# Softmax attention of a two-block transformer kernel: the last gate unit in halves through exp and ln, meta rows in a buffer of their own, the row maximum in two parts, transpositions between the scores

## The reference

```python
def gqa_block(q_blk, k, v):
    s = jnp.einsum('bkgqd,bksd->bkgqs', q_blk, k).astype(jnp.float32) * (HEAD_DIM ** -0.5)
    p = jax.nn.softmax(s, axis=-1)
    return jnp.einsum('bkgqs,bksd->bkgqd', p.astype(v.dtype), v)
...
        a_out = attention_branch(q, k, v, q_norm_g[i], k_norm_g[i], cos, sin, n_tok) * jax.nn.silu(a_gate)
```

## Time and profile before

| | us |
|---|---|
| median of 3 runs | 2239.23 |
| lowest and highest | 2237.02, 2241.11 |
| the profiled execution, its own time | 2239.75 |
| its span in the profile | 2238.0 |
| TensorE busy | 2123.8 |
| VectorE busy | 1104.5 |
| ScalarE busy | 831.3 |
| GpSimd busy | 746.5 |

### The profile page before, as it was taken

How to read it: one execution, slowest core, us unless ns; L and a number is a source line. 1 busy time by engine, 2 the same in 40 slices (tenths; PEclk the granted TensorE clock), 3 DMA queues, 4 the chain that set the end, 5 groups by cost and what they waited for, 6 DMA issues and landing times.

```text
span 2238.0 us, 27665 instructions
## 1 busy us (share of the span) xinstructions
PE 2123.8 (95%) x10545; PEld 1752.9 (78%) x10545; DVE 1104.5 (49%) x1483; ACT 831.3 (37%) x1482; POOL 746.5 (33%) x660
## 2 busy tenths in 40 slices
PE   5899998999998999999999999989999999999996
PEld 4687887999776778787877888868888888878785
DVE  7347656787434276766656743442222223221523
ACT  5133226888323264554545532431222122111212
POOL 3222141222232422222322334223333333366662
PEclk8999998999999999999999999999999999999998
DMA  5031130010132211111212443421111111132432
GB/s 171 26 123 52 48 94 27 10 48 10 55 113 81 66 58 52 53 61 52 79 42 80 155 141 124 132 76 47 47 47 47 47 47 47 47 113 94 148 106 76
DMA packets 142923, 164.68 MB, mean 74 GB/s; under 512 B 7092, under 2 KB 109000, under 8 KB 142824
## 3 DMA queue, kind: packets, MB, share of 16 engines
q1 hardware_dynamic: 118663, 98.10, 14.4%
q10 hardware_dynamic: 24160, 65.23, 8.3%
HBM read 133.94 MB, written 29.36 MB: 73 GB/s over the span
## 4 chain that ended last, share of the span: by engine, by line
PE 83%; DVE 10%; ACT 3%; issue 2%; DMA 1%; ACTq 0%; POOL 0%; DVEq 0%; POOLq 0%
PE psum L660 18%; PE psum L662 18%; PE psum L661 18%; PE psum L973 14%; PE psum L876 3%; PE psum L887 3%; PE psum L906 1%; PE psum L907 1%; PE psum L1010 1%; PE psum L908 1%; DVE softplus_part L2103 1%; PE psum L994 1%; DVE xn L1814 1%; PE psum L995 1%; PE psum L1027 1%
## 5 line engine op out<-in xcount | busy, mean ns | idle before, releaser
L557 POOL TENSOR_TENSOR w_ring<-w_staging,zero 128x8 fp32r<-128x8 f32 x172 | 44.3, 258 | 1227.6 <-PE psum L662 758.1
L560 POOL TENSOR_TENSOR w_ring<-w_staging,w_ring 128x1024 fp32r<-128x1024 f32 (+1 forms) x172 | 444.9, 2587 | 14.4
L973 PE MATMUL psum<-h,w_ring 128*128 128x512 f32 x1728 | 433.6, 401 | 0.7 <-ACT v L1489 0.7
L973 PEld LDWEIGHTS psum<-h,w_ring 128*128 128x128 f32 x1728 | 317.2, 190 | 67.6 <-ACT v L1489 1.1
L660 PE MATMUL psum<-ffn_in,w_ring 128*128 128x512 f32 x672 | 265.8, 395 | 0.0
L662 PE MATMUL psum<-ffn_in,w_ring 128*128 128x512 f32 x672 | 264.5, 394 | 0.0
L661 PE MATMUL psum<-ffn_in,w_ring 128*128 128x512 f32 x672 | 264.2, 393 | 0.0
L2236 DVE SCALAR_TENSOR_TENSOR up_buf<-psum,vectors,up_buf 128x1023 f32<-128x1023 f32 x44 | 56.5, 1283 | 308.2 <-ACT up_buf L1710 308.2
L558 POOL TENSOR_SCALAR w_ring<-w_staging 128x1016 fp32r<-128x1016 f32 (+1 forms) x172 | 183.8, 1069 | 0.0
L662 PEld LDWEIGHTS psum<-ffn_in,w_ring 128*128 128x128 f32 x672 | 126.1, 188 | 30.4
L661 PEld LDWEIGHTS psum<-ffn_in,w_ring 128*128 128x128 f32 x672 | 126.4, 188 | 29.0
(11 more groups left out here) (277 smaller groups left out, 4495.5 us busy)
## 6 DMA issues: line engine op xcount, KB each, us to landing
w_staging<-in_w_in SPq DMA_DIRECT2D x58, 512.0 KB, 3.8
w_staging<-in_w_up SPq DMA_DIRECT2D x44, 512.0 KB, 3.8
w_staging<-in_w_down SPq DMA_DIRECT2D x44, 512.0 KB, 3.2
w_staging<-in_w_out SPq DMA_DIRECT2D x16, 512.0 KB, 3.8
scratch_gates<-gate_out ACTq DMA_DIRECT2D x32, 256.0 KB, 2.3
merge_gates<-scratch_gates ACTq DMA_DIRECT2D x16, 512.0 KB, 4.5
x_again<-scratch_x ACTq DMA_DIRECT2D x16, 512.0 KB, 4.5
xin<-in_x ACTq DMA_DIRECT2D x8, 512.0 KB, 3.3
```

What stands on the lines that cost most here:

```text
L560: pool.tensor_tensor(lo[:, 0:width], WS[:, s, 0:width], plain(hi[:, 0:width]), ALU.subtract).then_inc(S["w_split"], 1)
L973: ins = pe.matmul(mix_bank(h), (sl if x == 2 else sh)[:, P * k:P * k + P], ml if x == 1 else mh, start=m == 0, stop=m == UNIT // 2 - 1)
```

## The change

- The last gate unit is made in halves: for each half of the tokens ScalarE takes exp of minus the value, ln of one plus that, and exp of minus that (the sigmoid from functions of the table that the softmax uses), into a buffer gate_e3 of its own. The first half is done in step 1 ahead of its exp, the second at the end of step 3. VectorE multiplies halves in steps 1 and 4. TensorE waits for the first half before attend of step 3 and for the second before that of step 5. The store goes out in step 5; only the load for head 6 waits for it. The sigmoid and both table loads of step 2 go.
- The copy in place behind each gate's product on VectorE goes; a store waits for the product.
- Meta rows of the transposed probabilities get a buffer probs_t_meta outside u. GpSimd clears it once the queries are all transposed. The split of chunk C_OUT+3 moves behind the meta rows of step 1.
- The maximum is taken over banks 0 and 1, then over bank 2, then the smaller of the two negatives by a third instruction on 128x1 elements.
- TensorE's step becomes: scores of banks 0 and 1, transpositions of group 0, scores of bank 2, transpositions of groups 1 and 2, attend.

```diff
@@ -280,7 +280,7 @@
         ZERO = at("zero", [P, 8], c0 + 688)
-        NB = at("minus_max", [P, 2], c0 + 424)
+        NB = at("minus_max", [P, 6], c0 + 424)
         IDR = at("ident_r", [P, P], c0 + 432, F32R)
@@ -340,7 +340,9 @@
         OT = at("attended", [P, 4, PAIR], T0 + 3624)
-        PT = at("probs_t", [P, 2, KTILES, 4 * P], R1, F32R)
+        PT = at("probs_t", [P, 2, TT, 4 * P], R1, F32R)
+        PTM = at("probs_t_meta", [P, 4 * P], T0 + 4648, F32R)
+        GE3 = at("gate_e3", [P, N_TOK], T0 + 5168)
         MIXA = at("mixed_a", [P, 2, 4, N_TOK], R1 + 9216, F32R)
@@ -365,7 +367,7 @@
         CAUSALR = at("causal_raw", [P, P], c1 + 2056)
-        ONE = at("one", [P, 1], c0 + 416)
+        ONE = at("one", [P, 2], c0 + 416)
@@ -560,8 +562,9 @@
+            pool.memset(ONE[:, 1:2], 1.0).then_inc(S["zero_set"], 1)
             pool.memset(ZERO[:, :], 0.0).then_inc(S["zero_set"], 1)
-            pool.wait_ge(S["zero_set"], 1)
+            pool.wait_ge(S["zero_set"], 2)
             peeled = C_KV + 4
@@ -591,7 +594,8 @@
-            run(peeled, C_OUT + 4, 1)
+            run(peeled, C_OUT + 3, 1)
+            pool.wait_ge(S["w_split"], C_OUT + 3)
@@ -607,8 +611,8 @@
-            pool.wait_ge(S["w_used"], C_OUT)
-            pool.memset(plain(PT[:, 0, TT, :]), 0.0).then_inc(S["pt_zero"], 1)
+            pool.wait_ge(S["pr_t"], KTILES + TT)
+            pool.memset(plain(PTM[:, :]), 0.0).then_inc(S["pt_zero"], 1)
             pool.wait_ge(S["pt_zero"], 1)
@@ -617,9 +621,12 @@
                     pool.wait_ge(S["o_lo"], (i - 10) // 2 + 1)
-                pool.tensor_scalar(PT[META_VLO:META_VLO + META, 0, TT, t], plain(PT[0:META, 0, TT, t]), 1.0, 0.0,
+                pool.tensor_scalar(PTM[META_VLO:META_VLO + META, t], plain(PTM[0:META, t]), 1.0, 0.0,
                                    ALU.mult, ALU.add).then_inc(S["pt_meta"], 1)
                 pool.wait_ge(S["pt_meta"], i + 1)
+                if i == 1:
+                    run(C_OUT + 3, C_OUT + 4, 1)
+                    pool.wait_ge(S["w_split"], C_OUT + 4)
                 if i >= 6 and i % 2 == 0:
@@ -724,6 +731,8 @@
                             ins.then_inc(S["w_used"], 1)
+                        elif c == C_AGATE + 3 and k == KT - 1:
+                            ins.then_inc(S["gate3_half"], 1)
                         if between is not None:
@@ -866,20 +875,21 @@
-            def scores(i):
+            def scores(i, parts=range(3)):
                 h, t = divmod(i, TT)
-                for b in range(3):
+                for b in parts:
                     if i:
...
                                         k2[:, h // GROUP, KPART * b:KPART * (b + 1)], start=x == 0, stop=x == 1)
-                ins.then_inc(S["sc_mm"], 1)
-
-            def turn_probs(i):
+                    if b:
+                        ins.then_inc(S["sc_half" if b == 1 else "sc_mm"], 1)
+
+            def turn_probs(i, groups=range(3)):
                 pe.wait_ge(S["sc_exp"], 3 * i + 3)
-                for g in range(3):
+                for g in groups:
                     if i:
@@ -907,7 +917,7 @@
                 if part:
-                    pe.matmul(dst, VV[0:META_ROWS, TT, g, 0:P], PT[0:META_ROWS, 0, TT, PAIR * (p % 2):PAIR * (p % 2) + PAIR],
+                    pe.matmul(dst, VV[0:META_ROWS, TT, g, 0:P], PTM[0:META_ROWS, PAIR * (p % 2):PAIR * (p % 2) + PAIR],
                               start=False, stop=True).then_inc(S["av_mm"], 1)
@@ -921,10 +931,16 @@
                 if i < HEADS * TT:
-                    scores(i)
+                    scores(i, range(2))
                 if i <= HEADS * TT:
-                    turn_probs(i - 1)
+                    turn_probs(i - 1, range(1))
+                if i < HEADS * TT:
+                    scores(i, range(2, 3))
+                if i <= HEADS * TT:
+                    turn_probs(i - 1, range(1, 3))
                 if i == 3:
+                    pe.wait_ge(S["gate_half"], 1)
+                elif i == 5:
                     settle(fm=U_AGATE + 4)
@@ -1359,8 +1375,21 @@
+            def a_gate_half(h):
+
+                if h:
+                    act.wait_ge(S["w_used"], C_AGATE + 4)
+                else:
+                    act.wait_ge(S["gate_stored"], 96)
+                    act.wait_ge(S["zero_set"], 2)
+                    act.wait_ge(S["gate3_half"], 1)
+                e = GE3[:, FW * h:FW * h + FW]
+                link(act.activation(e, PB[:, 2 * A_GATE_PAIRS[3] + h, :], ACT.Exp, scale=-1.0))
+                link(act.activation(e, e, ACT.Ln, bias=ONE[:, 1:2]))
+                act.activation(e, e, ACT.Exp, scale=-1.0).then_inc(S["gate3_sig"], 1)
+
             def store_a_gate(f):
-                act.wait_ge(S["gate_out"], 4 + f + 1)
+                act.wait_ge(S["fm_free"], U_AGATE + f + 1)
                 act.dma_start(scratch["a_gate"][P * f:P * f + P, :], GE2[:, f % 2, :]).then_inc(S["gate_stored"], 16)
@@ -1376,6 +1405,8 @@
                 r = DH * (h % 2)
+                if h == 6 and c == 0:
+                    act.wait_ge(S["gate3_stored"], 16)
                 act.dma_start(AG[r:r + DH, b % 2, :], scratch["a_gate"][DH * h:DH * h + DH, FW * c:FW * c + FW])\
@@ -1386,11 +1417,11 @@
                     act.wait_ge(S["pt_mm"], n + 1)
-                    rows = P if g < 2 else META
-                    kts = slice(4 * g, min(4 * g + 4, KTILES))
-                    act.activation(PT[0:rows, 0, kts, P * t:P * t + P],
-                                   PB[0:rows, 3 + g, 0:P * (4 if g < 2 else 1)].rearrange("p (k n) -> p k n", n=P),
-                                   ACT.Copy).then_inc(S["pt_hi"], 1)
+                    if g == 2:
+                        act.activation(PTM[0:META, P * t:P * t + P], PB[0:META, 5, 0:P], ACT.Copy).then_inc(S["pt_hi"], 1)
+                    else:
+                        act.activation(PT[:, 0, 4 * g:4 * g + 4, P * t:P * t + P],
+                                       PB[:, 3 + g, :].rearrange("p (k n) -> p k n", n=P), ACT.Copy).then_inc(S["pt_hi"], 1)
@@ -1409,15 +1440,15 @@
             for i in range(HEADS * TT):
+                if i == 1:
+                    a_gate_half(0)
                 if i == 2:
+                    act.wait_ge(S["w_used"], C_OUT)
                     act.wait_ge(S["pt_zero"], 1)
                     probs_hi(0)
-                    a_gate(3)
-                    load_tables()
-                if i == 4:
-                    store_a_gate(3)
                 if i == 5:
-                    act.wait_ge(S["gate_stored"], 112)
+                    act.wait_ge(S["fm_free"], U_AGATE + 4)
+                    act.dma_start(scratch["a_gate"][3 * P:4 * P, :], GE3[:, :]).then_inc(S["gate3_stored"], 16)
                     load_a_gate(0)
@@ -1428,6 +1459,8 @@
                     probs_hi(i - 1, range(2, 3))
+                if i == 3:
+                    a_gate_half(1)
                 if i >= 5 and i % 2:
@@ -1994,8 +2027,12 @@
                 v.tensor_tensor(e, pair(A_GATE_PAIRS[f]), e, ALU.mult).then_inc(S["fm_free"], 1)
-                v.wait_ge(S["fm_free"], 4 + f + 1)
-                v.tensor_scalar(e, e, 1.0, None, ALU.mult).then_inc(S["gate_out"], 1)
+
+            def a_gate_half(h):
+
+                e = GE3[:, FW * h:FW * h + FW]
+                v.wait_ge(S["gate3_sig"], h + 1)
+                v.tensor_tensor(e, PB[:, 2 * A_GATE_PAIRS[3] + h, :], e, ALU.mult).then_inc(S["fm_free" if h else "gate_half"], 1)
@@ -2006,31 +2043,37 @@
                 for g in groups:
-                    rows = P if g < 2 else META
-                    kts = slice(4 * g, min(4 * g + 4, KTILES))
                     v.wait_ge(S["pt_hi"], 3 * i + g + 1)
-                    lo = PT[:, 1, kts, P * t:P * t + P] if g < 2 else PT[META_LO:META_ROWS, 0, kts, P * t:P * t + P]
-                    v.tensor_tensor(lo,
-                                    PB[0:rows, 3 + g, 0:P * (4 if g < 2 else 1)].rearrange("p (k n) -> p k n", n=P),
-                                    plain(PT[0:rows, 0, kts, P * t:P * t + P]), ALU.subtract).then_inc(S["pt_lo"], 1)
+                    if g == 2:
+                        v.tensor_tensor(PTM[META_LO:META_ROWS, P * t:P * t + P], PB[0:META, 5, 0:P],
+                                        plain(PTM[0:META, P * t:P * t + P]), ALU.subtract).then_inc(S["pt_lo"], 1)
+                    else:
+                        kts = slice(4 * g, 4 * g + 4)
+                        v.tensor_tensor(PT[:, 1, kts, P * t:P * t + P], PB[:, 3 + g, :].rearrange("p (k n) -> p k n", n=P),
+                                        plain(PT[:, 0, kts, P * t:P * t + P]), ALU.subtract).then_inc(S["pt_lo"], 1)
...
                 if p == 0:
-                    v.wait_ge(S["gate_stored"], 112)
+                    v.wait_ge(S["gate_stored"], 96)
                 if p >= 4:
...
             for i in range(HEADS * TT):
+                first, last = (NB[:, 2 + 2 * (i % 2) + x:3 + 2 * (i % 2) + x] for x in range(2))
```

(14 more changed lines are left out.)

4 lines of the change are left out of this document (2 added, 2 removed).

## The result

| us | before | after |
|---|---|---|
| median of 5 runs each | 2239.23 | 2227.63 |
| lowest and highest | 2237.02, 2243.26 | 2225.14, 2229.91 |
| the profiled execution | 2239.75 | 2228.94 |
| its span | 2238.0 | 2227.1 |
| scores of step 2 start | 336.65 | 335.99 |

The account below looks back on a forecast made before the run. TensorE, busy 95% of the span, bounds the kernel; only its idle and slowed time in the softmax stage can change. Entry 9.6 plus steady 1.5 make 11.1 off the profiled 2239.75: about 2228.5 us, range 2222.5 to 2236, chance .42.

Parts of the forecast that it names:

- The entry: Start of the softmax stage: scores of step 5 at 349.19 instead of 358.79, a gain of 9.6 us.
- The steady gain: Softmax steps after the entry: 29 pairs of steps, each slightly shorter, 1.5 us gained, bounds 4.4 either way.
- The gate half: Second gate half on ScalarE after step 3's exp: three linked passes over 512 elements, 1.9 to 2.0 us, partly covered.
- The maximum by parts: VectorE's maximum: .88 us for two banks, .515 for one, .16 for the minimum; its start .30 earlier in steady state.
- The two roads to the exp: Steady state: one exp is reached through the maximum or ScalarE's high parts, both at 430.60; a shorter maximum gives little.
- the .05 per pair: Steady state: after the long attend the exp comes at 430.55 instead of 430.60; .15 worse or better as bounds.
- Rival 1: Entry: GpSimd's split holds the minimum of step 3 through the shared port; 2.35 us lost, 2231; chance .30.
- Rival 2: Softmax steps: the maximum's parts do not overlap, .3 to .33 more per step; slower, 2249; chance .06.
- Rival 3: Steady state: all bubbles vanish, .4 us per pair, 12 us gained, 2218 with the entry; chance .05.
- Rival 4: Entry: TensorE's clock falls there too, slowing transpositions and attends; 4 to 5 us lost, 2233; chance .10.
- The table loads: Entry: two loads of 1.28 us go, 2.57 together; with the skill's drain 5.3, and up to 2.8 more gain.
- Rival 5: Entry: its wait is replaced by another, leaving the time within 2 us of before; chance .07.

Follow-up runs that it names:

- kernel 5: Kernel after with the old last gate unit (sigmoid between two table loads, in step 2); new meta buffer and GpSimd order stay; 2236.06 us, ratio 0.9971.
- kernel 6: Kernel after with GpSimd's old order, clearing the meta buffer behind the split and the gate unit's last matmul; 2234.50 us, ratio 0.9971.
- kernel 2: Kernel before with only the two steady edits: maximum in parts, transpositions between the scores; 2239.44 us, ratio 0.9989.
- kernel 4: Kernel after with the maximum in one instruction, TensorE's new order kept; 2244.16 us, ratio 1.0005.
- kernel 7: Kernel after with GpSimd's postponed split behind the meta rows of step 0 instead of step 1; 2230.83 us, one run.
- kernel 3: Kernel after with all scores ahead of all transpositions again, the maximum still in parts; 2231.45 us, ratio 0.9949.
- kernel 9: Kernel after with all high parts, meta rows included, ahead of ScalarE's exp and all low parts in one piece on VectorE; 2231.25 us, ratio 0.9962.
- kernel 8: Kernel after with one pass instead of three in the second gate half, so the gate is not computed; 2225.11 us, one run.
- kernel 10: Kernel after with the second gate half at the end of step 2 instead of step 3; 2228.94 us, ratio 0.9948.
- kernel 1: Kernel after with one maximum and TensorE's old order, so the entry's edits only; 2233.12 us, ratio 0.9954.

## Why the prediction was right

It said 2228.5 and 2227.63 came. That the two are within 1 us is in part luck. The entry was priced rightly. The steady gain came 1.7 us larger than the sum has it, and .66 ahead of the entry is in no term; against that the profiled execution lost 2.9 again behind the last exp, which is in no term either (below). The entry's walk against the trace after:

| start of | predicted | after |
|---|---|---|
| scores of step 2 | 336.65 | 335.99 |
| high parts of step 0 | 336.98 | 336.19 |
| exp of step 2 | 340.65 | 340.00 |
| exp of step 3 | 344.1 | 343.45 |
| second gate half | 345.7 | 344.92 |
| exp of step 4 | 348.58 | 347.76 |
| scores of step 5 | 349.19 | 348.37 |

- **Entry, 9.6 predicted, 9.76 measured.** All rows are early by .65 to .82, of which .66 is the earlier start. The gate half was put at 1.9 to 2.0 and took 1.98 from its first pass to the end of its last.
- **Why it works** needed both edits. The prediction added the gains as one walk and did not say that neither would do alone; kernels 5 and 6 beside kernel 2 show it.
- **The maximum by parts**: .88 and .515 from a line through other reductions, 882 and 509 ns measured; the minimum .16, as said. The .15 from a maximum's end to the exp was wrong: .03 where ScalarE is free (kernels 4 and 7), so the maximum had more slack than the walk gave it.
- **Steady state, 1.5 predicted, 3.2 measured.** Half of the mechanism held. The two roads to the exp are there: kernel 3 shows that the one over the high parts binds, kernel 9 that .15 more on it costs the whole gain. But the prediction put the gain to the maximum's start, .30 earlier, as well, and that gives nothing by itself (kernel 3). The gain is the shorter road over the high parts, through TensorE's order; the parts keep the maximum from becoming the later road (kernel 4). The term that was mis-sized is the .05 per pair. It was .10 to .11 (7.23 to 7.13). The step behind the long attend gained the .05 (scores to exp 2.53, from 409.46 to 411.99, against 2.58); the rest is TensorE's way from the end of an exp to the next scores, which the walk put at 3.25 (424.80 to 428.05) and which takes 3.19. The walk took the interleaved order to be a stall of .03 worse than the old one; it is .03 better. That is within the bounds of .15.
- **Rival 1**, the minimum held by GpSimd, was missed by .13 us (343.25 against 343.38) where .2 was predicted. Kernels 5, 7 and 9 show that the hold is real: the minimum takes 1.56, 1.79 and 1.00 us. A miss of .13 in a walk that is good to .3 is luck as much as foresight. It was the same in the profiles of kernels 3, 8 and 10, .12 to .13.
- **Rival 2**, parts that do not overlap: wrong. The first maximum starts .85 after the scores of its step (410.31, 409.46), where the old one started 1.18 after them: .33 of lead for .30 predicted. VectorE is free just in time for it.
- **Rival 3**, all bubbles gone: wrong; the road over the high parts stayed, as said against it.
- **Rival 4**, the clock: 1.00 through the entry. The Trainium skill (TensorE: Matmul & The Clock Gate, A second HAM failure mode) describes a clock that swings on small idles between groups of matmuls; here idles of .86, 1.45 and .47 with work between them did not bring it down. Where it did fall, in kernels 5 and 6, the entry was 6.9 us longer, the wait ahead of the fall included; the 4 to 5 put there were for the clock alone, and TensorE's busy time there was 3.0 and 3.6 longer.
- **The table loads.** The prediction took 1.28 each, against the drain of 1.38 beside each load that the Trainium skill has (ScalarE: Activation LUTs, What ACT_TABLE_LOAD costs). Kernel 5 shows gate and loads back to back, from 338.48 to 342.09, with nothing beside the 1.28. The trace does not show such a drain.
- **Rival 5**, that it doesn't do what it says: no wait took the old one's place.

One thing the prediction did not have: in the profiles not all of the gain arrives. Up to the last exp the profiled executions differ by 13.6 us, at the end by 10.8. From the last exp to the last matmul the kernel before took 1646.5 and the kernel after 1649.4, though nothing there was changed. Part of it is in the windows of after, against those of before around the same work:

```profile
778.00:782.00 4.00, 3.98 (x12) 3.31 (x13) 3.46 (x5) 2.70 (x4) 0.00 (x0) 0.57 0.44 128
```

```profile
791.00:795.00 4.00, 4.00 (x22) 3.39 (x22) 3.26 (x5) 2.59 (x5) 0.00 (x0) 1.00 0.36 108
```

TensorE comes out of an idle of 2.29 us at 778.02 and runs at a mean clock of 0.57, with 12 matmuls in 4 us; before, it comes out of one of 2.28 us at 790.80, runs at 1.00 and starts 22. Another such stretch, at 0.50, lies at 1072 to 1075. In the profiles of the ten experiments the same part took 1647.2 to 1652.6 us, so it varies by more than the 2.9 between the two, and the single profile of before is below all the others. The part goes with the time at half clock in it. Between the last exp and 2200 us the traces have:

| us at a granted clock of 0.50 | kernels | last exp to last matmul |
|---|---|---|
| 30.6 | before, 2, 4, 7, 8 | 1646.5 to 1648.1 |
| 34.0 | after, 6, 9, 10 | 1649.3 to 1649.9 |
| 37.4 | 1, 3 | 1651.3 |
| 40.8 | 5 | 1652.6 |

Kernels 7 and 8 have the whole of the change but for a place and two passes, and stand in the first row with the kernel before. So the 2.9 us are a difference between executions as far as these traces show, and no cost of the change; each kernel has one profile, so whether the change makes such falls likelier is not settled. The medians differ by 11.6, and the interval of the ratio, 10.5 to 15.7, has room for the whole 13.6.

## What to carry to other kernels

When TensorE waits for a chain with two blocks in it, price the removal of each with the other still there: here the clock fell as long as either stayed, and each alone gave 1.5 us where both gave 8.4. Splitting the reduction paid here only with the matmuls reordered, and the reordering lost without the split; find the second road to the same start (here ScalarE's high parts) before pricing either. And the largest wait in the list is not the next thing to remove: look first whether what it releases starts late.

## What was not expected of the hardware

- The granted clock does not follow an idle's length alone. Idles of 3.07, 3.48 and 5.15 us in the entry were followed by 0.50 in kernels 7, 5 and 6, for some 3 us in the first and some 10 us in the others, which have a further idle within these 10 (2.27 in kernel 5, .91 in kernel 6); an idle of 2.29 was followed by a fall in one execution, and one of 2.28 at the same work in another was not.
- VectorE's minimum of two 128x1 operands in SBUF, started beside GpSimd's split, ends when the split does, within .02 us: 1.56, 1.79 and 1.00 us for 0.16. It missed that by .13 us in the kernel after, so a small shift of either engine can cost 1.6 us. A subtraction with one operand in PSUM beside the same split (343.33 in the kernel after) took its usual 1.28 for two.
- A pass of ln over 512 elements whose bias is a column of ones takes 0.72 us, the pass of exp behind it 0.63, and exp out of PSUM 0.57.
